# A first output projection by blocks of 512 tokens with the second norm beside it, and another order at the edge of a recurrence step

## What is computed

```
h = rms_norm(x, norm)                      # first block
...                                        # projections, decay, state recurrence over tokens
y = group_norm(y) ... * g                  # (T, 1024), from the recurrence
x2 = x + y @ w_out                         # first output projection, residual
h2 = x2 * rsqrt(mean(x2 * x2) + 1e-6) * norm_w_2     # second norm
proj = h2 @ w_in_2                         # second block goes on from h2
out = x2 + concat(y_conv, y_attn) @ w_out_2
```

## Time and profile before

| | us |
|---|---|
| median of 3 runs | 3454.93 |
| lowest, highest | 3451.9, 3457.21 |
| profiled execution | 3456.85 |
| its span | 3455.1 |
| mean granted TensorE clock | 0.922 |

### The profile page before, as it was taken

The page is one execution under the profiler, slowest core; times in us unless marked ns, Lnnn a source line. Parts: engine busy times, 40 slices in busy tenths (PEclk is TensorE's granted clock), DMA queues, the critical chain, the costliest instruction groups (busy, mean ns, idle before and its releaser), DMA issues. The chain is left out here.

```text
span 3455.1 us, 78976 instructions
## 1 busy us (share of the span) xinstructions
PE 2966.5 (86%) x35142; PEld 2450.5 (71%) x35142; DVE 1574.4 (46%) x2593; ACT 1068.4 (31%) x1976; POOL 526.2 (15%) x350
## 2 busy tenths in 40 slices
PE   4699999998768878887874984999899997999799
PEld 1587888886467777777773862888777786777587
DVE  4424232432166666766743116222247601777663
ACT  2223332322534435434432014111022211545410
POOL 0222222210022222222210000000000000034221
PEclk8799999999969888989986997999999998999899
DMA  5213331211633233233214331111011223322672
GB/s 156 79 49 115 98 116 55 85 53 46 218 108 101 64 88 100 65 88 97 56 28 158 122 115 61 33 34 33 34 55 61 75 72 125 133 77 88 205 241 93
DMA packets 312098, 318.37 MB, mean 92 GB/s; under 512 B 12847, under 2 KB 231343, under 8 KB 310112
## 3 DMA queue, kind: packets, MB, share of 16 engines
q1 hardware_dynamic: 282512, 250.97, 23.5%
q10 hardware_dynamic: 26208, 54.55, 4.4%
q0 software_dynamic: 3056, 8.05, 1.0%
HBM read 195.57 MB, written 122.64 MB: 92 GB/s over the span
## 5 line engine op out<-in xcount | busy, mean ns | idle before, releaser
L424 PE MATMUL pj_ps<-pj_x_hi,pj_w_hi 128*128 128x512 f32 x1024 | 402.5, 393 | 72.1 <-DVE pj_x_lo L379 62.2
L424 PE MATMUL pj_ps<-pj_x_lo,pj_w_hi 128*128 128x512 f32 x1024 | 401.4, 392 | 0.0
L424 PE MATMUL pj_ps<-pj_x_hi,pj_w_lo 128*128 128x512 f32 x1024 | 401.3, 392 | 0.0
L424 PEld LDWEIGHTS pj_ps<-pj_x_hi,pj_w_hi 128*128 128x128 f32 x1024 | 194.1, 190 | 116.5 <-DVE pj_x_lo L379 63.4
L358 POOL TENSOR_TENSOR pj_x<-h 128x512 f32<-128x512 f32 x128 | 168.0, 1313 | 581.5 <-DVE pj_x_lo L379 519.0
L379 DVE TENSOR_TENSOR pj_x_lo<-pj_x,pj_x_hi 128x512 fp32r<-128x512 f32 x128 | 89.2, 696 | 360.2 <-ACT pj_x_hi L434 360.2
L424 PEld LDWEIGHTS pj_ps<-pj_x_hi,pj_w_lo 128*128 128x128 f32 x1024 | 194.1, 190 | 40.8
L424 PEld LDWEIGHTS pj_ps<-pj_x_lo,pj_w_hi 128*128 128x128 f32 x1024 | 194.1, 190 | 40.3
L2168 DVE CUSTOM_DVE_ANT_0 wa_sc<-wa_sps,wa_table 128x256 f32<-128x256 f32 (+2 forms) x384 | 124.1, 360 | 144.2 <-PE wa_sps L2099 144.1
L1644 PE MATMUL cv_ps<-h_hi,cv_w_hi 128*128 128x512 f32 x512 | 158.7, 391 | 23.9 <-DVE cv_w_lo L1687 23.9
L885 ACT CAST rw_x<-rw_ps 128x512 f16<-128x512 f32 x160 | 96.1, 601 | 203.6 <-PE rw_ps L1180 203.5
(11 more groups left out here) (260 smaller groups left out, 6442.3 us busy)
## 6 DMA issues: line engine op xcount, KB each, us to landing
proj<-pj_out ACTq DMA_DIRECT2D x128, 256.0 KB, 2.5
pj_w<-w_in SPq DMA_DIRECT2D x32, 512.0 KB, 4.3
proj<-lr_out SPq DMA_DIRECT2D x32, 512.0 KB, 4.7
partial<-wa_ob SPq DMA_DIRECT2D x48, 264.0 KB, 2.1
mo_part<-partial SPq DMA_DIRECT2D x16, 792.0 KB, 8.6
wa_vt<-v_rows SPq DMA_DIRECT2D x43, 260.0 KB, 3.5
h<-xT SPq DMA_DIRECT2D x8, 1024.0 KB, 12.8
proj<-pj_scaled ACTq DMA_DIRECT2D x32, 256.0 KB, 3.3
```

The lines of the kernel that those rows point to most:

```text
L424: mm = pe.matmul(ps[i][:], wp, xp, start=k == 0 and m == 0, stop=k == KT - 1 and m == len(parts) - 1)
```

## The change

Three edits. In the recurrence: `m_add` is split off as `m_sum` and stands between the two transposes; the new state of the second chunk is computed in the next step; the last two evictions of `a` move behind the masks of level one in the next step; TensorE asks for `m_add` only ahead of the half that writes bank 1, and the merges of level one go ahead of `y_from_tokens`. `output_projection` and `split_norm_phase` go, and `normed_output` does the work of both: four blocks of 512 tokens, 8 rows (output groups) in a block, the norm of a block beside the products of the next. `early_hi` and `early_lo` are float views of the memory of `h2_hi` and `h2_lo`; y is loaded into the one, x2 written into the other. Weight tiles are loaded once per block, with the transfer three rows ahead. Squares are summed over row groups on GpSimd into `acc`, and one product by ones gives the total; the root is exp(-0.5 ln(.)) on ScalarE, in PSUM. The diff, without the bodies of the two removed functions:

```diff
@@ -1008,9 +927,10 @@
                     if f:
                         f.need("yt")
                     n.did(dve.tensor_tensor(y16[:, g], lt_less[:, g], over_heads(seed16[:]), ALU.mult), "seed")
-                for g in range(2):
-                    n.need("seed", g + 1)
-                    n.did(dve.transpose(wide(x16, g), wide(y16, g)), "turned")
+            def turn_seed(n, g):
+                n.need("seed", g + 1)
+                n.did(dve.transpose(wide(x16, g), wide(y16, g)), "turned")
             def decay_sums(n, i):
                 n.need("in_sw")
@@ -1032,9 +952,11 @@
                 f.did(dve.tensor_copy(u_tok[f.t % 2][chunk(ci), 0].rearrange("p j t -> p (j t)"),
                                       PS[chunk(ci), UB[0], :]), "u_sb0")
-            def m_next(f, ci):
+            def m_sum(f, ci):
                 f.need("m", ci + 1)
                 f.did(dve.tensor_tensor(mtmp[:], bank(MB, RW_N), state(f.t, ci)[:], ALU.add), "m_add")
+            def m_next(f, ci):
                 f.need("m_add", ci + 1)
                 f.need("dec")
                 f.did(dve.tensor_tensor(state(f.t, ci + 1)[:], mtmp[:],
@@ -1046,6 +968,9 @@
                     n.did(dve.tensor_scalar(kss[:], PS[0:64, 6, 0:128], 1e-24, None, ALU.max), "kmax")
                 if f:
                     masked(f, 1)
+                    a_evict(f, 3)
+                if b:
+                    m_next(b, 1)
                 if n:
                     decay_sums(n, 0)
                     decay_sums(n, 1)
@@ -1112,6 +1037,7 @@
                 if n:
                     less_unit(n, f, 0)
                 if f:
+                    m_sum(f, 0)
                     m_next(f, 0)
                 if n:
                     a_evict(n, 1)
@@ -1121,9 +1047,11 @@
                     half_u(f, 1)
                 if n:
                     seeds(n, f)
-                    a_evict(n, 3)
-                if f:
-                    m_next(f, 1)
+                    turn_seed(n, 0)
+                if f:
+                    m_sum(f, 1)
+                if n:
+                    turn_seed(n, 1)
             run(dve, step)
@@ -1153,10 +1081,12 @@
                 at = C_AT["selectT"] + 128 * i
                 return cst[P, at:at + 128]
-            def products(f, l):
+            def products(f, l, b=None):
                 for g in range(2):
                     if l == 1:
                         f.need("turned", g + 1)
+                        if b and XB[g] == MB:
+                            b.need("m_add")
                     else:
                         f.need("xy_sb", 2 * (l - 2) + g + 1)
                     for j in range(KT):
@@ -1323,17 +1253,14 @@
             def step(n, f, b):
                 if f:
                     if b:
-                        b.need("m_add")
                         b.need("u_sb0")
                         b.need("u_sb1")
-                    products(f, 1)
+                    products(f, 1, b)
+                    merges(f, 1)
                 if b:
                     if f:
                         f.need("a_sb")
                     y_from_tokens(lambda R, g, j: v_tok[b.t % 2][R, j, rows(g)], mat_k[b.t % 2], True)
-                if f:
-                    merges(f, 1)
-                if b:
                     b.need("u_sb0")
                     b.need("u_sb1")
@@ -1417,152 +1344,247 @@
+def normed_output(nc, src, w_out, residual, dst, gain, h2_hi, h2_lo, early_hi, early_lo):
+    NB, BANKS, RING = T // 512, 6, 3
+    STEPS = NB * KT
     with ExitStack() as c:
         sems = Semaphores(nc, c)
...
         w = [sb(f"w{i}", [128, KT, 128]) for i in range(2)]
+        w_hi, w_lo = ([sb(f"{n}{i}", [128, KT, 128], F32R) for i in range(RING)] for n in ("w_hi", "w_lo"))
+        y_hi, y_lo = (sb(n, [128, KT, 512], F32R) for n in ("y_hi", "y_lo"))
+        res = [sb(f"res{i}", [128, 512]) for i in range(RING)]
+        acc, ones = sb("acc", [128, 512]), sb("ones", [128, 128])
+        sq = [sb(f"sq{i}", [128, 512]) for i in range(2)]
+        eps = sb("eps", [128, 1])
+        ps = [c.enter_context(nc.psum_tensor(f"no_ps{i}", [128, 512], F32)) for i in range(BANKS)]
+        var = [c.enter_context(nc.psum_tensor(f"no_var{i}", [128, 512], F32)) for i in range(2)]
...
+        def y_in(b, k):
+            return early_hi[:, k, cols(b)]
+        def x2(b, j):
+            return early_lo[:, j, cols(b)]
         @block.sync
         def _(sp):
+            def load_w(n):
+                if n >= 2:
+                    sp.wait_ge(s_w_lo, n - 1)
+                j = n % KT
+                sp.dma_start(w[n % 2][:], w_cols[:, :, 128 * j:128 * j + 128]).then_inc(s_w[n % 2], 16)
+            def load_y(b, k):
+                sp.dma_start(y_in(b, k), src_v[:, k, cols(b)]).then_inc(s_y[k], 16)
+            def load_res(n):
+                sp.dma_start(res[n % RING][:], res_v[:, n % KT, cols(n // KT)]).then_inc(s_res[n % RING], 16)
+            def store(n):
+                b, j = n // KT, n % KT
+                sp.wait_ge(s_sum, n + 1)
+                sp.dma_start(dst_v[:, j, cols(b)], x2(b, j)).then_inc(s_out[j], 16)
+                if n + RING < STEPS:
+                    load_res(n + RING)
+            load_w(0)
+            for k in range(KT):
+                load_y(0, k)
+                if k == 3:
+                    load_w(1)
+            load_w(2)
+            for n in range(RING):
+                load_res(n)
+            for n in range(STEPS):
+                if n + 3 < STEPS:
+                    load_w(n + 3)
+                if n % KT == 0 and n + KT < STEPS:
+                    sp.wait_ge(s_y_lo, n + KT)
+                    for k in range(KT):
+                        load_y(n // KT + 1, k)
+                if n:
+                    store(n - 1)
+            store(STEPS - 1)
+            for j in range(KT):
+                sp.wait_ge(s_out[j], 16 * NB)
+        @block.gpsimd
+        def _(pool):
+            pool.memset(ones[:], 1.0).then_inc(s_ones, 1)
+            pool.memset(eps[:], EPS).then_inc(s_ones, 1)
+            for b in range(NB):
+                for j in range(1, KT):
+                    n = b * KT + j
+                    pool.wait_ge(s_square, n + 1)
+                    if j > 1:
+                        pool.wait_ge(s_acc, (KT - 1) * b + j - 1)
+                    pool.tensor_tensor(acc[:], acc[:], sq[n % 2][:], ALU.add).then_inc(s_acc, 1)
         @block.scalar
         def _(act):
+            def weights(n):
+                if n >= RING:
+                    act.wait_ge(s_mm, n - RING + 1)
+                act.wait_ge(s_w[n % 2], 16 * (n // 2 + 1))
+                act.copy(w_hi[n % RING][:], w[n % 2][:]).then_inc(s_w_hi, 1)
+            def y_high(b, k):
+                if b:
+                    if k == KT - 1:
+                        act.wait_ge(s_mm, KT * b)
+                    else:
+                        act.wait_ge(s_y_free, (KT - 1) * (b - 1) + k + 1)
+                act.wait_ge(s_y[k], 16 * (b + 1))
+                act.copy(y_hi[:, k, :], y_in(b, k)).then_inc(s_y_hi, 1)
+            def square(n):
+                b, j = n // KT, n % KT
+                act.wait_ge(s_sum, n + 1)
+                if j == 0:
+                    act.wait_ge(s_total, b)
+                    target = acc
+                else:
+                    act.wait_ge(s_acc, (KT - 1) * b + max(j - 2, 0))
+                    target = sq[n % 2]
+                act.activation(target[:], x2(b, j), ACT.Square).then_inc(s_square, 1)
+            def root(b):
+                act.wait_ge(s_total, b + 1)
+                act.activation(var[b % 2][:], var[b % 2][:], ACT.Ln, scale=1.0 / D, bias=eps[:]).then_inc(s_log, 1)
+                act.wait_ge(s_log, b + 1)
+                act.activation(var[b % 2][:], var[b % 2][:], ACT.Exp, scale=-0.5).then_inc(s_inv, 1)
+            def high(b, k):
+                act.wait_ge(s_scaled, KT * b + k + 1)
+                act.copy(h2_hi[:, k, cols(b)], x2(b, k)).then_inc(s_high, 1)
+            act.preload_act_table_set("natural_log_exp_and_others")
+            weights(0)
+            for k in range(KT):
+                y_high(0, k)
+            weights(1)
+            for n in range(STEPS):
+                b, j = n // KT, n % KT
+                if n + 2 < STEPS and j < KT - 1:
+                    weights(n + 2)
+                if n:
+                    square(n - 1)
+                if b and j == 1:
+                    root(b - 1)
+                if b and 2 <= j < 6:
+                    high(b - 1, 2 * (j - 2))
+                    high(b - 1, 2 * (j - 2) + 1)
+                if j == KT - 1 and b + 1 < NB:
+                    for k in range(KT):
+                        y_high(b + 1, k)
+                    weights(n + 2)
+            square(STEPS - 1)
+            root(NB - 1)
+            for k in range(KT):
+                high(NB - 1, k)
         @block.tensor
         def _(pe):
+            def total(b):
```

(76 more changed lines are left out.)

195 lines of the change are left out of this document (13 added, 182 removed).

## The result

| us | before | after |
|---|---|---|
| median (lowest to highest) | 3456.07 (3451.9 to 3462.97) | 3346.19 (3329.16 to 3358.26) |
| ratio, 95% interval | | 0.9665 [0.9635, 0.9696] |
| profiled execution, its span | 3456.85, 3455.1 | 3351.66, 3349.6 |
| untouched stages ahead of the recurrence | 942.4 | 939.0 |
| recurrence, first transfer to last store | 879.9 | 874.3 |

Faster by 3.35%. The ratio puts the changed kernel at 3339.2 on the scale of the forecast: 3 us under the low end of the range (3342) and 21 under the forecast. The gain was forecast at 95 us; by the ratio it is 116 (by the plain medians 110, and 110 to 117 in the three sets of runs that follow).

What follows compares the result with a forecast made beforehand. TensorE was taken as busy only in the products (176 us), idle in the load and nearly so in the norm. 3456.85 - 88.9 (join) - 6 (recurrence) = 3361.95; the median 1.9 lower, so 3360, range 3342 to 3384.

Steps and rivals of the forecast that it cites:

- Three stages in sequence, joined: Output projection and norm: load, products and norm overlap instead of following each other; 88.9 us less, all reaching the end.
- Start: Join's beginning: first product 7.9 us after the first transfer, plus 1.8 for low clock and 1.0 for arriving pieces.
- Rows: Join: 5.44 us for each row of 24 products, 174.2 in all; norm work and transfers beside them cost nothing.
- Rival 2: Join: VectorE sets the row beside norm work, 8.0 us a row, 2.6 over in 12 rows: 3391; chance 0.08.
- Edges: Three block edges in the join: TensorE idles 3.0 us for `total`, then 1.13 and 1.6: 5.7 each, 17.1 together.
- Tail: Join, after the last row: final sum, root, scalings and subtractions without products beside them, 17.5 us.
- Recurrence: Wait on `m_add` divided, not removed, by the new order: 0.4 us gained a tile, 15 times, 6 in all.
- two ends: Recurrence, outputs done: 0.9 us sooner at full clock, 0.4 later at half; 13 gained or 6 lost in all.
- a tile shorter by under 1 us: Recurrence: expected sign in the trace of the forecast gain; 2 us and more would have meant rival 1.
- rival 1: Recurrence: the 39.8 us of waits on `m_add` vanish whole because the evictions hide: 3326; chance 0.07.
- rival 3: Edges or clock cost more than counted and the order in the recurrence loses: 3375 to 3384; chance 0.12.
- rival 5: Join: the norm doesn't run beside products, a wait costing some 20 us three times: 3404; chance 0.02.

Runs made afterwards that it cites:

- rec_only: The kernel before with the new order in the recurrence alone, output projection and norm as before: 3441.5 us (before, same chip: 3461.95).
- stage_only: The kernel before with the new joined output projection and norm alone, recurrence as before: 3362.27 us (before, same chip: 3461.95).
- evict_first: The changed kernel with the last two evictions of `a` back ahead of the masks of level one: 3365.25 us (before, same chip: 3461.95).
- evict_alone: The changed kernel with VectorE's new order in the recurrence but TensorE's old one: 3363.7 us (before, same chip: 3448.32).
- total_row1: The changed kernel with `total` one row later, behind row 1 of the next block, and sums of squares in separate tiles: 3333.52 us (before, same chip: 3458.78).
- w_twice: The changed kernel with every weight tile also copied once more in device memory: 3358.64 us (before, same chip: 3458.78).

## Right and wrong, step by step

- **Three stages in sequence, joined.** Right. Join 213.0 against a forecast of 219.5; what follows it took 1318.8 us (1319.4 before), so the gain came off one for one.
- **Start.** 7.6 us to the first product, forecast 7.9. Row 0 at half clock until some 3.3 us in; the row waits 0.46 us once for weights.
- **Rows.** 5.44 us each, as forecast (the last two sums start at 2009.63 and 2015.07). Rival 2 fell: VectorE is busy 114 of 190 us. Its one trait that is real, the contention, shows at the edges.
- **Edges.** The term was mis-sized: 5.7 each, 17.1 in all. First product to last sum took 189.6 us; less the 174.2 of products, the 1.8 of the start and 0.5 of waiting for weights it leaves 13.1, 4.4 an edge. Idle was 2.07 in the mean, not 3.0, and the low clock followed only two of three (one of three in each of the three repeats of the changed kernel). The kind of wait, its place and its releaser were right.
- **Tail.** 15.7 us (2015.07 to 2030.75), forecast 17.5. A scaling and a subtraction take 1.26 us from start to start, where I had added their durations to 1.43.
- **Recurrence.** The step that failed: 0.4 us a tile, 6 in all, where the traces show 0.84 and 12.7 and the medians 17 (10 to 24). I had put the gain between two ends, 0.9 at full clock and -0.4 at half. Both ends were too low. Against the mean of the old order the new one gains 1.4 at full clock, and at the lower clock it does not lose 0.4, it gains 0.6. Three things make this up. The one edge that I had read was 0.2 shorter than the mean of the old order's 30 (outputs done 9.65 us behind the copy of u, against 9.86). The outputs begin 6.06 us behind the copy, not 6.35: I had added full durations in VectorE's queue. And at the lower clock I let both groups of outputs run at it, 3.66 us, where they took 3.23 in the mean, since a spell covers only 2.5 of it. The weight of the low clock was not too large: about 0.4 in my sum, while 121 of 180 edges of the new order had it. The direction of the wait was right: the one for `m_add` (37.2 us) is gone, and 24.8 at three places are left, 12.4 less. The sign "a tile shorter by under 1 us" came true, and rival 1 (the 40 us vanish whole) fell, as did rival 3, by which the new order loses, and rival 5.
- **What the sum did not hold.** The fourteen traces of kernels with the new join have the untouched projections, from first product to the first transfer of the next stage, at 717.0 to 721.3 us, 719.5 in the mean; the two without it (before and `rec_only`) at 723.3 and 726.1: some 5 us, in code that is the same. In the two, TensorE was idle for 11.9 and 14.1 us between products and at the lower clock for 13.7 in each; in the fourteen for 7.6 to 11.2 and 3.4 to 10.2. Two traces are few, and no run here took it apart: its cause stays open. Of the 21 us between forecast and result, the join has 6.5 (213.0 for 219.5), the recurrence 6.7 by the traces, and the projections 5; the rest is inside the scatter of the total.

## What to carry to other kernels

When an engine's queue decides at the edge of a loop, read that edge in every turn of the loop before pricing it: one edge, with one state of the clock, gave two bounds here that were too low by 0.5 and 1.0 us a tile, and a pair of edges from before and after can mix the change with the clock. A mean over like instructions can hide two values: ask what ran beside the long ones. An order change that moves work behind a wait on one engine pays only if the engine that waited gets other work for that gap: here either half of the swap alone was worth nothing. And measure a stage by its own first and last event: a join that repeats within 1.5 us could be read to 4 us in one trace, while the total time scatters by 20.

## What the runs showed of the hardware

The clock did not follow the length of the idle alone, nor the code. In seven traces of this same join (the changed kernel four times, `stage_only`, `evict_first`, `evict_alone`) the first and third edge had 1.99 to 3.25 us of idle; the clock fell to its lower level behind 9 of these 14 and not behind the other 5; it fell behind one idle of 1.99 us and not behind another, and not behind the 3.25. It fell behind none of the seven second edges, with 1.58 to 1.69. In `total_row1` it read 1.00 in every stretch of 3 us around gaps of 1.77 and 2.52 us. Of one program's 3350 us, the recurrence alone moved by 16 us between executions of the same code, the join by 1.1. A 128x512 subtraction with both inputs in SBUF took 0.68 us alone and, nine times of twelve, 1.35 beside a GpSimd addition of 1.3. And with the DMA engines busy all the time (`w_twice`), the join's transfers moved 295 to 303 GB/s over stretches of 47 to 49 us; over one of 3 us in the changed kernel the profile reads up to 375.
